# A two-block forward pass on one core: in the even layer, the last expert's results are copied earlier, a pair of tiles is combined between the parts of the pair ahead of it, and the next pair's turns stand one chunk earlier

## The reference, cut to what matters

```
y = zeros.at[slot_tok].add(yb * slot_gate)     # 32 experts, two results per token, weighted
x = x + y                                      # the combined rows, 1024 tokens x 1024
...
h_lat = layer_norm_2(x)   * (1 + scale)   + shift     # modulate: 1024 latent rows
h_ctx = layer_norm_2(ctx) * (1 + scale_c) + shift_c   # 256 context rows
z = einsum('bnd,de->bne', h, w_in)             # gq gk gv glr gg cq ckv kr mg, for both
```

## Time and profile before

| | us |
|---|---|
| median of 3 runs | 2549.76 |
| lowest, highest | 2548.52, 2550.42 |
| profiled execution: own time | 2549.97 |
| profiled execution: span | 2547.9 |
| PE busy | 2339.2 (92%) |
| DVE busy | 1529.2 (60%) |
| ACT busy | 1188.5 (47%) |
| POOL busy | 371.4 (15%) |

### The profile page before, as it was taken

The page is one execution under the profiler, slowest core; times in us unless marked ns, Lnnn a source line. Parts: engine busy times, 40 slices in busy tenths (PEclk is TensorE's granted clock), DMA queues, the critical chain, the costliest instruction groups (busy, mean ns, idle before and its releaser), DMA issues.

```text
span 2547.9 us, 27450 instructions
## 1 busy us (share of the span) xinstructions
PE 2339.2 (92%) x11068; PEld 1728.6 (68%) x11068; DVE 1529.2 (60%) x1877; ACT 1188.5 (47%) x1669; POOL 371.4 (15%) x258
## 2 busy tenths in 40 slices
PE   6988889798799999999879999988999999899998
PEld 5766555484488888888668677554555567778876
DVE  4766158544699999999761114756555637533475
ACT  3255246511488888888653144435444532312231
POOL 2000012000111111111100000001655534000014
PEclk9999999898799999999989999988999999899999
DMA  3210010117899999999641010010000022121141
GB/s 117 66 33 34 0 67 1 67 75 282 327 376 381 384 381 398 395 394 379 242 160 42 20 33 18 1 38 1 1 1 34 17 116 77 42 66 50 39 163 56
DMA packets 98874, 342.08 MB, mean 134 GB/s; under 512 B 21276, under 2 KB 46661, under 8 KB 71096
## 3 DMA queue, kind: packets, MB, share of 16 engines
q1 hardware_dynamic: 87096, 318.76, 33.5%
q0 software_dynamic: 10448, 17.28, 1.8%
q10 hardware_dynamic: 1200, 4.24, 0.4%
HBM read 323.41 MB, written 33.60 MB: 140 GB/s over the span
## 4 chain that ended last, share of the span: by engine, by line
PE 82%; DVE 9%; ACT 5%; DMA 2%; issue 2%; SPq 0%; POOL 0%; DVEq 0%; ACTq 0%; POOLq 0%
PE psm L230 78%; PE psm L1722 1%; DVE mem L953 1%; DMA mem<-in_ada_w_dram 1%; DVE r L337 1%; PE psm L1073 1%; PE psm L464 1%; ACT mem L1143 1%; PE psm L1745 1%; DVE mem L1187 1%; DVE mem L2735 1%; DMA mem<-in_odd_w_out_dram 1%; DMA mem<-in_w_in_dram 1%; ACT mem L1109 0%; DVE small L3002 0%
## 5 line engine op out<-in xcount | busy, mean ns | idle before, releaser
L230 PE MATMUL psm<-r,r 128*128 128x512 f32 (+4 forms) x7438 | 1783.1, 398 | 80.1 <-DVE r L337 22.6
L230 PEld LDWEIGHTS psm<-r,r 128*128 128x128 f32 (+3 forms) x7438 | 1385.9, 189 | 475.9 <-issue 62.0
L337 DVE TENSOR_TENSOR r<-mem,r 128x1024 fp32r<-128x1024 f32 x448 | 524.7, 1218 | 175.6 <-ACT r L328 170.1
L328 ACT ACTIVATE r<-mem 128x1024 fp32r<-128x1024 f32 x448 | 441.4, 1053 | 32.6 <-DMA mem<-in_w_in_dram 21.8
L230 PE MATMUL psm<-mem 128*64 128x128 f32 (+13 forms) x2230 | 362.8, 442 | 34.9 <-ACT mem L816 10.1
L230 PEld LDWEIGHTS psm<-mem 128*64 128x64 f32 (+6 forms) x2230 | 170.9, 165 | 157.3 <-issue 88.1
L3210 POOL TENSOR_TENSOR mem<-mem 128x1024 f32<-128x1024 f32 x63 | 153.9, 2443 | 177.6 <-ACT mem L3165 176.9
L3165 ACT ACTIVATE mem<-psm 128x512 f32<-128x512 f32 x160 | 95.3, 596 | 148.7 <-PE psm L230 141.2
L3002 DVE TENSOR_REDUCE small<-psm 128x1 f32<-128x1280 f32 x64 | 95.2, 1488 | 104.7 <-PE psm L230 104.3
L230 PE MATMUL psm<-mem,cst 128*128 128x512 f32 (+4 forms) x274 | 115.0, 638 | 23.0 <-ACT mem L924 5.5
L265 ACT ACTIVATE small<-small 128x1 f32<-128x1 f32 (+3 forms) x26 | 7.7, 296 | 246.2 <-DVE small L374 160.4
(11 more groups left out here) (338 smaller groups left out, 1769.8 us busy)
## 6 DMA issues: line engine op xcount, KB each, us to landing
mem<-in_exp_w_gate_dram SPq DMA_DIRECT2D x64, 1024.0 KB, 7.4
mem<-in_exp_w_up_dram SPq DMA_DIRECT2D x64, 1024.0 KB, 7.8
mem<-in_exp_w_down_dram SPq DMA_DIRECT2D x64, 1024.0 KB, 7.3
mem<-in_ada_w_dram SPq DMA_DIRECT2D x16, 1024.0 KB, 14.0
mem<-in_odd_w_in_dram SPq DMA_DIRECT2D x10, 1024.0 KB, 5.4
mem<-in_even_w_in_dram SPq DMA_DIRECT2D x9, 1024.0 KB, 5.5
mem<-in_x_dram SPq DMA_DIRECT2D x16, 512.0 KB, 7.0
mem<-in_w_in_dram SPq DMA_DIRECT2D x8, 1024.0 KB, 5.4
```

Source lines behind the costliest of these rows:

```text
L230: return p.e.matmul(o, l, r, start=start, stop=stop, skip_group_check=True)
L328: p.e.activation(h, mem(kb + 8, [R * n])[:, w * q:w * q + w], ACT.Copy).then_inc(*self.hi_done.up(i, q))
L337: p.e.tensor_tensor(l, mem(kb + 8, [R * n])[:, w * q:w * q + w], h.bitcast(F32), SUB).then_inc(*self.lo_done.up(i, q))
```

## The change

Four edits, with no instruction added or taken away, on any engine:

1. ACT: the two copies of the last expert's results go ahead of the context's scaling and hi parts of chunks 4 to 7.
2. ACT and DVE: the split of weight piece 0 goes ahead of the parts of chunks 0 to 3 of the context.
3. DVE: from pair 0 on, a tile of the next pair is combined ahead of each half of a pair's lo parts, where it stood behind it.
4. PE: the turns of the next pair's chunks 0 to 3 go ahead of chunk 6 instead of chunk 7.

```
@@ experts_scalar, last expert
                     turn_hidden_scalar(p, e)
                     WV.split_scalar(p, 1)
-                    nC.split_scalar(p, 0, CTX_ORDER[0:4])
                 for q in range(2):
@@ context_vector
             WV.split_vector(p, 1)
-            nC.split_vector(p, 0, CTX_ORDER)
+            nC.split_vector(p, 0, CTX_ORDER[0:4])
             WV.split_vector(p, 0)
+            nC.split_vector(p, 0, CTX_ORDER[4:8])
 
         def context_scalar(p):
+            nC.split_scalar(p, 0, CTX_ORDER[0:4])
+            WV.split_scalar(p, 0)
             nC.split_scalar(p, 0, CTX_ORDER[4:8])
-            WV.split_scalar(p, 0)
             for i in range(2):
                 values_out(p, i)
 
         def even_norms_vector(p):
+
+            for i in range(2):
+                combine_vector(p, i)
+            nL.center_vector(p, 0)
+            nL.norm_vector(p, 0)
+            p.wait_ge(*moe_pool.at("moved", 7))
             for k in range(4):
-                for n_, i in enumerate(nL.part(k)):
-                    if k:
-                        nL.split_vector(p, k - 1, range(4 * n_, 4 * n_ + 4))
-                    combine_vector(p, i)
-                nL.center_vector(p, k)
-                nL.norm_vector(p, k)
-                p.wait_ge(*moe_pool.at("moved", 7))
-            nL.split_vector(p, 3)
+                for n_ in range(2):
+                    if k < 3:
+                        combine_vector(p, 2 * k + 2 + n_)
+                    nL.split_vector(p, k, range(4 * n_, 4 * n_ + 4))
+                if k < 3:
+                    nL.center_vector(p, k + 1)
+                    nL.norm_vector(p, k + 1)
@@ values_by_chunks
             for n_, c in enumerate(order):
-                if n_ == 7 and then is not None:
+                if n_ == 6 and then is not None:
                     nL.turn_tensor(p, then, range(4), order=TURN_BANKS)
```

## The result

| | before | changed |
|---|---|---|
| median, us | 2549.14 (4 runs, 2547.45 to 2550.42) | 2533.23 (4 runs, 2532.38 to 2537.69) |
| profiled execution, own time, us | 2549.97 | 2532.38 |
| span, us | 2547.9 | 2530.5 |
| PE busy, us | 2339.2 | 2328.4 |

The ratio is 0.9945, with a 95% interval of 0.9933 to 0.9958: faster by 0.55%. The medians differ by 15.9 us. The forecast was 2531, in a range of 2528 to 2537.

A forecast was written before the change was run, and what follows sets the result against it. PE bounds the kernel, so only its waits ahead of mg count. Head 5.2, pair 0 1.2 to 2.9, pairs 1 and 2 4.7 each, pair 3 1.5: 18.9 us off 2549.97, so 2531, range 2528 to 2537.

The forecast's parts named there:

- The place and the measure: Between last expert and mg: PE is on the chain unbroken from 1353.82, so moving that moment moves the end equally.
- The head: From the last expert to pair 0's norm: first combine at 1265.1 against 1268.35, 5.2 us of the gain in all.
- DVE ... takes 2.36, so it ends at 1260.9: DVE's split of weight piece 0, ahead of chunks 0 to 3: claimed to take 2.36 us, ending at 1260.9.
- with the 0.2 us of the branch: On DVE between the last context lo part and the first combine: the overflow branch was to cost 0.2 us.
- Copies first: ACT after the last expert: scatter 3.6 us earlier, tile 0 landing at 1262.6, first lo 1.9 us later.
- Pair 0: First pair, PE restarting at half clock: saves 1.2 to 2.9 us, with 2.0 us taken for the slow clock.
- three restarts: Earlier PE restarts in the trace, full clock after 3.1 to 6.1 us, used to price pair 0's slow clock.
- Pairs 1 and 2: Middle pairs: 13.5 us each instead of 18.2 at full clock, saving 4.7 us each.
- the clock keeps falling: Rival, 18%: small waits drop PE's clock in every pair, 1.5 to 3 us each over three pairs, 2535 to 2540.
- the combine ahead of the lo parts binds: Rival, 8%: PE waits in each pair for lo parts behind DVE's combine, 1.5 to 3 us each, 2534 to 2540.
- Pair 3 and mg: Last pair to the projection: last turn 11.5 us after the norm instead of 13.0, then 6.8 to mg, saving 1.5.
- a late first load: The first combine's tile load landing late, by 1.1 to 2.5 us; 2533 if 2.5 us late.

The follow-up runs named there:

- poolw: Changed kernel with POOL's copies of tiles 6 and 7 held until DVE has split weight piece 0; ratio 0.9943 to the kernel before.
- early: Changed kernel with DVE's register load for the overflow branch moved ahead of the split of weight piece 0; ratio 0.9938 to the kernel before.
- late_copies: Changed kernel with the last expert's results copied behind the parts of chunks 4 to 7 again; ratio 0.9927 to the kernel before.
- filled: Changed kernel plus unread matmuls on PE: 20 behind its overflow branch, 12 between pair 0's turns and chunk 0; ratio 0.9932 to the kernel before.
- turns7: Changed kernel with the next pair's turns ahead of chunk 7 again instead of chunk 6; ratio 0.9942 to the kernel before.
- both: Changed kernel with POOL's copies held until the piece 0 split is done and DVE's register load moved earlier; ratio 0.9928 to the kernel before.
- behind: Changed kernel with tiles combined behind each half of the lo parts again; ratio 1.0003 to the kernel before.
- warm: Changed kernel plus 36 unread matmuls on PE behind the context's values, ahead of its overflow branch; ratio 0.9947 to the kernel before.
- allthree: Changed kernel with POOL's copies held, DVE's register load earlier and 36 unread matmuls ahead of PE's overflow branch; ratio 0.9931 to the kernel before.
- all: Changed kernel with POOL's copies held, DVE's register load earlier and 20 plus 12 unread matmuls around pair 0's turns; median 2529.72 us, ratio 0.9927.
- head: Kernel before with only the results copied first and weight piece 0 split ahead of chunks 0 to 3; ratio 0.9983 to the kernel before.

## Why the prediction was right, point by point

**The place and the measure: right.** From mg on PE is on the chain without a break after as before, and no wait appeared behind 1335: neither trace has PE waiting in the 223 us behind mg, other than 1.3 us for the split at its start.

**The head: a term of the sum too large.** I had the first combine 3.25 us earlier; counted from S it came 0.94 earlier (20.73 against 21.67). The step "DVE ... takes 2.36, so it ends at 1260.9" failed: it took 3.26, with POOL's copies of tiles 6 and 7 beside it, which edit 1 had moved there. `poolw` gave it back. The step "with the 0.2 us of the branch" failed: it was 1.27, because the branch had been worked through under the split, two instructions of 1.2 us each that waited for nothing new, and now stood behind a lo part that waits for ACT. `early` gave back 0.92 of it. That leaves 2.31 - 0.90 - 1.06 = 0.35: 0.1 ahead of the split, and the rest in small waits of ACT and DVE in the parts of chunks 0 to 3. The rest of the head held: copies done 6.36 after S (forecast 6.37), first lo at 7.30 (7.27), and the combine to N(0) 9.0. That PE's context chunks would no longer matter held too.

**Copies first: right in the times, without a gain in this kernel.** The load of tile 0 landed 15.8 after S (forecast 15.9). But I counted the edit as part of the head's gain, and `late_copies` shows that without it the first combine comes 0.8 us earlier. One part of its price, the 1.9 us delay of the first lo, stood in the same paragraph; the other, POOL's copies beside the split, did not. By my own sum the edit was needed: I had the combine 18.4 after S, and without the edit the load lands 19.9 after S. With the two costs the combine came at 20.73, later than either landing, so the early load bought nothing.

**Pair 0: right in the mechanism, and lucky in the size.** 15.52 against 15.5, with 1.92 of clock against 2.0, which `filled` shows to be the clock. The size varies: 14.96 to 16.40 in the nine traces with edit 3 and without the second fill, so 1.4 to 2.8 us of clock, where I had 1.6 to 2.4. Five of the nine lie above that range and one below. I had it from "three restarts"; the same trace has three more stretches at or near half clock, in pairs 1, 2 and 3, of 2.7, 3.5 and 6.2 us, and I left them out. What sets the size in an execution stays open.

**Pairs 1 and 2: right**, 13.60 and 13.61 against 13.5, at full clock, and the same in all runs with edit 3. The rival "the clock keeps falling" falls, and so does "the combine ahead of the lo parts binds". The Trainium skill's sentence on the throttle (TensorE: Matmul & The Clock Gate, What's actually happening) had it the right way: with waits of 0.19 us PEclk stayed at 1.00.

**Edit 4: not separated in the prediction.** I wrote of the turns at 3.0 us behind the last one, as if that place were needed. `turns7` shows that it isn't: norm and parts of the next pair set the pace either way.

**Pair 3 and mg: right**, 18.41 against 18.3.

**The sum.** I said 18.9 us. S to mg gave 16.27: less by the 2.3 of the head, and 0.3 of small rest. The median came 2.2 above the forecast for it. It lies in the range, but I had left the room up to 2537 for a late first load, a cold pair 0 and rivals, and not for the two costs that used it, so that too is in part luck. The two profiled executions differ by 17.4 in span: 16.27, plus the 2.55 by which S came early, less 1.4 lost behind mg, in the fall of the clock that is described below. So N(1) to N(3) and mg stood so close to the forecast because S came 2.55 early and the head lost 2.31. Why S came early is seen in part: 48 matmuls near 656, with the same work in both, took 10.65 us at PEclk 0.50 in the kernel before's execution and 5.64 at PEclk 1.00 in the changed kernel's. S lies between 1244.1 and 1249.1 in the 14 traces. The medians (15.9) fit the stage's gain.

## What to carry to other kernels

When work moves ahead on one engine, look at what it triggers on the others and what they will then run beside: 0.9 us of a 3.2 us gain went to a copy on another engine that used to run beside something else. Look too at what stands in front of a branch or register load: behind two long instructions it took 0.2 us here, behind a short one that waits 1.3. And a load that is brought forward is worth only what the next limit leaves of it: here nothing, behind a combine that was late for other reasons, and 1.0 us with those reasons gone (`late_copies` against `both`). So price the load against the new time of its reader, with all that the other edits cost it.

## What the runs showed of the hardware that was not expected

**DVE beside POOL.** Two subtractions of 128x1024 from SBUF took 3.20 to 3.26 us with POOL's two copies of 128x1024 beside them, and 2.36 without, in all runs of either kind. In three of them (`behind`, `warm`, `filled`) POOL's copies took longer too, 3.10 instead of 2.02. A lo part, whose first input is in PSUM, lost nothing beside the same copies: the one at 1261.55 in the kernel before took 0.43 us, where others took 0.42.

**A register load and a branch cost about 1 us on DVE when nothing hid them**: 1.27 us between two DVE instructions, 0.35 with the register load moved ahead, 0.21 behind the long split. On PE, 2.55 to 3.39 us of "issue" stand where the branch does, behind a run of matmuls (`warm`, `allthree`, `filled`, `all`); without the fills PE waited there anyway. The parts of this time on PE were not told apart.

**The clock falls behind a few narrow matmuls without any idling.** Some 181 us behind mg stand six matmuls whose inputs have 16 partitions only. In the changed kernel's run, PE was busy throughout, and PEclk was 0.50 for 3.4 us behind them; the timeline:

```profile
1511.62 4.95 PE L230 MATMUL psm<-r,r 128*128 128x512 f32 x21
1516.51 2.41 PE L230 MATMUL psm<-mem 16*128 16x256 f32 x6
1518.85 7.54 PE L230 MATMUL psm<-r,r 128*128 128x512 f32 x25
```

It fell there in 8 of the 14 traces and stayed full in 6, among them the kernel before. Each fall costs about 1.5 us (the PE stretch from mg on took 223.81 against 222.28). It is part of why single executions differ by some us. What decides it was not tried. Of the 11 traces with edit 3 it fell in 8, of the 3 without (before, `head`, `behind`) in none; with one trace of each kernel that can be chance, and a link with the edit is neither shown nor ruled out.
